# The recurrent block of layer 1 moved ahead of its memory attention, with two sets of gate buffers and a rearranged block loop

## The reference, cut to what matters

```python
def lru_mixer(h, w_in, conv_w, conv_b, wa, ba, wx, bx, lam):
    p = h @ w_in
    xb, gate, mq = jnp.split(p, [LRU_WIDTH, 2 * LRU_WIDTH], axis=-1)
    xc = centred_depthwise_conv(xb, conv_w, conv_b)
    y = (rg_lru(xc, wa[0], ba[0], wx[0], bx[0], lam[0], False)
         + rg_lru(xc, wa[1], ba[1], wx[1], bx[1], lam[1], True))
    y = y * jax.nn.gelu(gate)
    return y, mq.reshape(B, S, MEM_HEADS, MEM_HEAD_DIM)

def rg_lru(x, wa, ba, wx, bx, lam, reverse):
    r = jax.nn.sigmoid(block_diag_linear(x, wa, ba).astype(jnp.float32))
    i = jax.nn.sigmoid(block_diag_linear(x, wx, bx).astype(jnp.float32))
    log_a = -LRU_C * r * jax.nn.softplus(-lam.astype(jnp.float32))
    a = jnp.exp(log_a)
    u = jnp.sqrt(-jnp.expm1(2.0 * log_a)) * (i * xf)
    _, h = lax.associative_scan(_linear_combine, (a, u), axis=1, reverse=reverse)
```

## Time and profile before

| engine | busy us | share of the span |
|---|---|---|
| PE (matmul) | 3663.4 | 91% |
| DVE | 1690.4 | 42% |
| POOL | 1210.8 | 30% |
| ACT | 974.2 | 24% |

### The profile page before, as it was taken

How to read it: one execution, slowest core, us unless ns; L and a number is a source line. 1 busy time by engine, 2 the same in 40 slices (tenths; PEclk the granted TensorE clock), 3 DMA queues, 4 the chain that set the end, 5 groups by cost and what they waited for, 6 DMA issues and landing times. The chain is left out here.

```text
span 4028.1 us, 45875 instructions
## 1 busy us (share of the span) xinstructions
PE 3663.4 (91%) x16526; PEld 2930.9 (73%) x16526; DVE 1690.4 (42%) x1834; ACT 974.2 (24%) x1547; POOL 1210.8 (30%) x650
## 2 busy tenths in 40 slices
PE   6788887999999997977579999999799999978999
PEld 4666665888888885755358888888568888856877
DVE  4324445163343345356634434333643343243454
ACT  2224444020101012343412110101143433312101
POOL 0111002233333331145543333333233443412350
PEclk9899998999999998988789999999899999989999
DMA  3100000221111112011012111111121111111332
GB/s 138 60 21 17 15 11 6 94 68 47 47 51 48 47 47 73 24 34 31 26 68 68 47 47 47 51 47 47 43 73 58 57 42 52 58 40 34 99 102 97
DMA packets 56409, 209.92 MB, mean 52 GB/s; under 512 B 6000, under 2 KB 10352, under 8 KB 55424
## 3 DMA queue, kind: packets, MB, share of 16 engines
q1 hardware_dynamic: 46352, 158.35, 12.8%
q10 hardware_dynamic: 9968, 50.43, 3.3%
HBM read 186.74 MB, written 22.02 MB: 52 GB/s over the span
## 5 line engine op out<-in xcount | busy, mean ns | idle before, releaser
L486 PE MATMUL G<-Hhi,whi 128*128 128x512 f32 x2752 | 1143.3, 415 | 96.5 <-ACT T L1015 33.2
L486 PE MATMUL G<-Hlo,whi 128*128 128x512 f32 x2752 | 1084.1, 394 | 0.0
L486 PE MATMUL G<-Hhi,wlo 128*128 128x512 f32 x2752 | 1083.6, 394 | 0.0
L358 POOL CAST whi<-wraw 128x1024 fp32r<-128x1024 f32 (+1 forms) x268 | 285.5, 1065 | 2465.7 <-PE G L486 1274.3
L486 PEld LDWEIGHTS G<-Hhi,whi 128*128 128x128 f32 x2752 | 524.7, 191 | 238.9 <-issue 87.4
L360 POOL TENSOR_TENSOR wlo<-wraw,whi 128x1024 fp32r<-128x1024 f32 (+1 forms) x268 | 665.3, 2482 | 21.5
L486 PEld LDWEIGHTS G<-Hlo,whi 128*128 128x128 f32 x2752 | 525.1, 191 | 118.7 <-issue 7.4
L486 PEld LDWEIGHTS G<-Hhi,wlo 128*128 128x128 f32 x2752 | 523.6, 190 | 112.0
L486 PE MATMUL G<-Uhi,whi 128*128 128x512 f32 x1024 | 398.8, 389 | 0.0
L486 PE MATMUL G<-Ulo,whi 128*128 128x512 f32 x1024 | 398.8, 389 | 0.0
L486 PE MATMUL G<-Uhi,wlo 128*128 128x512 f32 x1024 | 398.8, 389 | 0.0
(11 more groups left out here) (285 smaller groups left out, 4605.9 us busy)
## 6 DMA issues: line engine op xcount, KB each, us to landing
wraw<-wjobs SPq DMA_DIRECT2D x292, 512.0 KB, 3.5
X<-xT ACTq DMA_DIRECT2D x2, 4096.0 KB, 14.9
scratch<-X ACTq DMA_DIRECT2D x2, 4096.0 KB, 11.9
gate_tiles<-gate_st ACTq DMA_DIRECT2D x16, 512.0 KB, 2.7
T<-gate_tiles ACTq DMA_DIRECT2D x16, 512.0 KB, 3.3
X<-scratch ACTq DMA_DIRECT2D x1, 4096.0 KB, 13.2
X<-scratch SPq DMA_DIRECT2D x4, 1024.0 KB, 11.6
out<-yn ACTq DMA_DIRECT2D x8, 512.0 KB, 2.6
```

The costliest lines, as they stand in the source:

```text
L358: pool.tensor_copy(whi[:, par, 0:kt], wraw[:, par, 0:kt]).then_inc(w_hi, 1)
L486: mm = pe.matmul(G[:, par, cols], w[:, par, k, :], x[:, k, cols], start=(k == 0 and j == 0), stop=(k == kt - 1 and j == 2))
```

## The change

- The phases are reordered: the 16 jobs `lru` come first, then the 4 jobs `mq1`. `lru()` is called before `mem_attention(1)` on PE, ACT and DVE, and the weights lie in memory in that order.
- `rg` and `ig` exist twice (by the parity of the block). The gelu is written straight into `mixed`; `gl` is gone. `a*a` is no longer a square: ACT makes it by a second exponential with twice the constant (`decay_c[:, 96:112]`) into the tiles `lt`, one of which is `T[:, 1]`. So ACT has six activations of a whole tile per block there instead of four.
- POOL does no part of the recurrence any more: `ig * xc` goes to DVE, the square to ACT. POOL's list holds only weight splits through layer 1's mixer; `split_mixed` of six tiles comes after the last `mq1` job.
- ACT's block j: the second direction's sigmoids and the exponentials of block j-1, the gelu of j, the roots of j-1, the first direction's sigmoids of j, the copy of the input of j+1. DVE's block j: convolution of j, then the rest of j-1 (`behind`). PE's block j: job 2j+1, first gates of j, job 2j+2, second gates of j.
- In the last memory head, 12 of the 16 parts of the first `wo_mixed1` job are put between the attention's instructions. The four heads of layer 1 are written out instead of looped, and use `probs1` for `probs`.
- The six `split_mixed` wait for the end of all `mq1` jobs, since they overwrite `Hhi` and `Hlo`.

```diff
@@ PHASES
-    PHASES += [(f"mq{_l}", 4, "act")]
-    PHASES += [("k", 2, "act"), ("v", 2, "act"), ("q", 8, "act")] if _l == 0 else [("lru", 16, "act")]
+    PHASES += [("mq0", 4, "act"), ("k", 2, "act"), ("v", 2, "act"), ("q", 8, "act")] if _l == 0 else \
+              [("lru", 16, "act"), ("mq1", 4, "act")]
@@ POOL
-            splits(START["up00"], START["lru"] + 4)
+            splits(START["up00"], START["lru"] + 2)
...
-                for dr in range(2):
-                    pool.wait_ge(l_sig, j * 4 + (2 * dr + 2))
-                    pool.tensor_tensor(ig[:, dr], ig[:, dr], xc[par][:], ALU.mult).then_inc(l_ix, 1)
-                for dr in range(2):
-                    pool.wait_ge(l_exp, j * 4 + (2 * dr + 2))
-                    pool.tensor_tensor(T[:, dr], av[:, dr], av[:, dr], ALU.mult).then_inc(l_a2, 1)
...
+            splits(START["lru"] + 2, START["wo_mixed1"] + 2)
             pool.wait_ge(job_done, START["wo_mixed1"])
-            for k in range(3):
-                split_mixed(1, k, l_y, k + 1)
-            lru_block(7, 1, last=True)
-            for k in range(3, EARLY):
-                split_mixed(1, k, l_y, k + 1)
+            for k in range(EARLY):
+                split_mixed(1, k, l_y, 2 + k + 1)
@@ PE, mem_attention: the parts between in the last head
+                        if last:
+                            for q in range(max(2 * u - 4, 0), max(2 * u - 2, 0)):
+                                next_part(q, after, 1 - par, shift, (early_lo, EARLY * l))
@@ PE, lru
+                def block_of(j, i, par, ahead=True):
+                    for q in range(16):
+                        next_part(q, j * 2 + (START["lru"] + 1), 1, shift)
                     pe.wait_ge(l_xc, j + 1)
-                    pe.wait_ge(lw_in[par], lw_count * 16 + 16)
+                    pe.wait_ge(lw_in[par], i * 16 + 16)
+                    pe.wait_ge(l_sig, j * 4 + 4)
                     gates(par, 0)
...
+                            next_part(q, j * 2 + (START["lru"] + 2), 0, shift)
+                    pe.wait_ge(l_sig, j * 4 + 6)
+                    gates(par, 1)
@@ ACT, lru
+                def block_of(j, par, jm1, j1, j2):
+                    if jm1 is not None:
+                        sigmoids(jm1, 1 - par, 1)
+                        decays(jm1, 1 - par)
+                    gelu(j)
+                    if jm1 is not None:
+                        roots(jm1)
+                    sigmoids(j, par, 0)
+                    if j1 is not None:
+                        input_of(j1, 1 - par)
@@ DVE, lru
+                def behind(j, par, between=None):
+                    r, i = rg[par], ig[par]
+                    dve.wait_ge(l_sig, j * 4 + 8)
+                    for dr in range(2):
+                        dve.tensor_tensor(i[:, dr], i[:, dr], xc[par][:], ALU.mult).then_inc(l_ix, 1)
+                    for dr in range(2):
+                        dve.wait_ge(l_exp, j * 6 + (3 * dr + 3))
+                        dve.scalar_tensor_tensor(lt[dr][:], lt[dr][:], 1.0, r[:, dr], ALU.add, ALU.mult).then_inc(l_e, 1)
...
+                def block_of(j, par, jm1, x_ahead=True, g_ahead=True):
+                    convolve(j, par)
+                    behind(jm1, 1 - par)
```

More of the change, by code:

```diff
@@ L690, in project_out, with ready @@
             def project_out(l):
-                jobs(f"wo_mixed{l}", 8, Hhi, Hlo,
-                     lambda k: (early_lo, EARLY * l + k + 1) if k < EARLY else (split_lo[l], k - EARLY + 1))
+                name = f"wo_mixed{l}"
+                def ready(k):
+                    return (early_lo, EARLY * l + k + 1) if k < EARLY else (split_lo[l], k - EARLY + 1)
+                if l:
+                    for q in range(12, 16):
+                        job_part(q, START[name], 0, Hhi, Hlo, ready)
+                    psum_waits(name, 1, 1)
+                    job(START[name] + 1, 1, Hhi, Hlo, ready)
+                    with pe.Fori(1, 4) as i:
+                        for par in range(2):
+                            psum_waits(name, i * 2 + par, par)
+                            job(i * 2 + (START[name] + par), par, Hhi, Hlo, ready)
+                else:
+                    jobs(name, 8, Hhi, Hlo, ready)
                 jobs(f"wo_mem{l}", 8, MOhi, MOlo, (split_lo[l], KT - EARLY), kt=4)
@@ L733, in gates @@
                     mm.then_inc(l_mm, 1)
-                def first_gates(j, lw_count, par):
+                def block_of(j, i, par, ahead=True):
+                    for q in range(16):
+                        next_part(q, j * 2 + (START["lru"] + 1), 1, shift)
                     pe.wait_ge(l_xc, j + 1)
-                    pe.wait_ge(lw_in[par], lw_count * 16 + 16)
+                    pe.wait_ge(lw_in[par], i * 16 + 16)
+                    pe.wait_ge(l_sig, j * 4 + 4)
                     gates(par, 0)
[L740 to L745, removed]
                     if ahead:
                         for q in range(16):
[L748 to L755, removed]
+                            next_part(q, j * 2 + (START["lru"] + 2), 0, shift)
+                    pe.wait_ge(l_sig, j * 4 + 6)
+                    gates(par, 1)
+                psum_waits("lru", 0, 0)
+                job(START["lru"], 0, Hhi, Hlo, (norm_s["lo"], tiles_before("nmix1")))
+                pe.wait_ge(evac["dve"], 2 + BASE["lru"]["dve"])
                 with pe.Fori(0, 3) as i:
@@ L758, in lru @@
                         block_of(i * 2 + par, i, par)
-                block_of(6, 3, 0, ahead=False)
-                pe.wait_ge(l_sig, 30)
-                gates(1, 1)
+                block_of(6, 3, 0)
+                block_of(7, 3, 1, ahead=False)
             def gla():
@@ L1169, in input_of, with sigmoids @@
                     act.dma_start(lw[:, par], block).then_inc(lw_in[par], 16)
[L1171 to L1181, removed]
+                def sigmoids(j, par, dr):
+                    if dr == 0:
+                        act.wait_ge(l_y, j + 1)
+                    wait_apart(act, l_mm, j * 2 + (dr + 1))
+                    for g, (dst, b) in enumerate(((rg[par], "lru_ba"), (ig[par], "lru_bx"))):
+                        act.activation(dst[:, dr], AUX[:, 2 * g:2 * g + 2, :].rearrange("p a n -> p (a n)"),
+                                       ACT.Sigmoid, bias=dcol(b, j + 8 * dr)).then_inc(l_sig, 1)
@@ L1186, in block_of, with roots @@
+                def roots(j):
                     for dr in range(2):
                         act.wait_ge(l_e, j * 2 + (dr + 1))
-                        act.activation(T[:, dr], T[:, dr], ACT.Sqrt, scale=-1.0).then_inc(l_sq, 1)
-                    act.wait_ge(l_y, j + 1)
-                input_of(0, 0)
-                with act.Fori(0, 3) as i:
-                    for par in range(2):
-                        block_of(i * 2 + par, par)
-                block_of(6, 0)
-                block_of(7, 1, last=True)
+                        act.activation(lt[dr][:], lt[dr][:], ACT.Sqrt, scale=-1.0).then_inc(l_sq, 1)
@@ new lines, in gelu @@
+                def gelu(j):
+                    wait_apart(act, job_done, j * 2 + (L0 + 2))
+                    act.activation(tile_of(mixed, j), G[:, 1, :], ACT.Gelu_apprx_tanh).then_inc(evac["act"], 1)
+                def block_of(j, par, jm1, j1, j2):
[8 more added lines that the diff above has]
+                        input_of(j1, 1 - par)
@@ new lines, in lru @@
+                act.wait_ge(l_dx, 3)
+                input_of(0, 0)
+                block_of(0, 0, None, 1, True)
+                with act.Fori(0, 2) as i:
+                    block_of(i * 2 + 1, 1, i * 2, i * 2 + 2, True)
+                    block_of(i * 2 + 2, 0, i * 2 + 1, i * 2 + 3, True)
+                block_of(5, 1, 4, 6, True)
+                block_of(6, 0, 5, 7, False)
+                block_of(7, 1, 6, None, False)
+                sigmoids(7, 1, 1)
+                decays(7, 1)
@@ L1198, in gla @@
+                roots(7)
             def gla():
```

120 lines of the change are left out of this document (66 added, 54 removed).

## The result

Four runs of the changed kernel took 3914.3, 3917.45, 3920.78 and 3920.93 us, the median 3919.11; four of the kernel before beside them 4026.27 to 4029.1, the median 4028.41. The ratio is 0.9728, 95% interval 0.9711 to 0.9745: 109 us or 2.7% faster. The forecast was 3911.0, with a range of 3893 to 3945. The profiled run took 3920.78 us, its span is 3919.0.

A forecast was written before the change was run, and what follows sets the result against it. Waits among PE, ACT and DVE held the recurrence; seven periods shortened by 14.2 us (about 99), plus three POOL waits and two lone jobs, less the new open end, saved 117 us: 3911 us, range 3893 to 3945.

The forecast's parts named there:

- Period 29.0: One recurrence block takes 29.0 us, PE's own two jobs and two gates, instead of 43.2 us.
- DVE's 3 to 4 us idle before the roots: Sign in the recurrence blocks: DVE has about 3 to 4 us idle before the roots.
- The sums behind it: Work per recurrence block on other engines: DVE 24.6 us with two POOL splits, ACT 21.4 us with table loads.
- Step 1: Stage start: decay constants stand before the first copy, convolution ends at 1591, costing PE nothing to 1 us.
- step 4: Block 7, no job ahead: PE waits 5.6 us, gates cost up to 6.5, then a stall of 2.2.
- Steps 2 and 3: Block 0's gates and job end at 1609.1; blocks 1 to 6, 29.0 us each, end at 1783.1.
- Step 5: First memory job ends at 1822.8; first head's maximum, queued behind block 7 on DVE, is 5.7 us late at 1834.8.
- Step 6: Attention up to the last splits: 105.7 us plus 5.7 late, less 0.7 at the last head, reaching 1933.5.
- DVE as bound: Rival, 17%: DVE sets the recurrence period; 33 us gives 3939, the upper bound of 37.5 gives 3971.
- POOL late: Rival, 9%: in the last head PE waits 14 us for POOL's six splits, giving 3925 us.
- No overlap: Rival, 4%: recurrence blocks stay chained through ACT, the period stays near 43 us, giving 4010 us.
- The clock: Rival, 3%: PE gets the lower clock level over the stage, its work doubles, giving about 4210 us.

The follow-up runs named there:

- Chained_blocks: Changed kernel, but ACT waits for the last multiply of block j-1 before the gelu of block j: 3980.09 us, 0.9889 of the kernel before.
- Early_constants: Changed kernel, but DVE works out the decay constants in layer 0, long before the stage: 3906.72 us, 0.9706 of the kernel before.
- Second_job_first: Changed kernel, but PE runs memory job 0 before block 7's last gates and memory job 1 whole before head 0: 3911.71 us, 0.9719.

## Why the prediction was right, step by step

It named the mechanism and came within 8 us. On its own clock, from the first job's end to the last splits, it had 353.9 us and the profile has 359.3 (1940.78 less 1581.5, the end that POOL's mark at 1581.61 shows).

- *Period 29.0.* Right: 28.66, PE with no wait. Seven times 0.34 is 2 us on the other side. DVE's 3 to 4 us idle before the roots are 4.3 to 4.5. Chained_blocks shows that the overlap makes this. The sums behind it were too high: DVE is busy 20.8 us a block, not 24.6, so the splits cost it 1.6 us and not 5.4; ACT has 14 tiles a block and not 15, 19.8 us in all with the loads where I had 21.4.
- *Step 1, the step that failed.* "This costs PE nothing to 1 us": it cost 6.2 us of wait and 3.0 of slow gates, 9.2 us. I had taken the constants from a place with no POOL beside the earlier trace rows, 7.1 us with the table load, and a clean convolution of 4.7. Both overlapped a split: the constants end 10.1 us after they began (2.7 of it in the two slowed instructions), the convolution takes 7.4 with its first operation. And the lower level on gates behind a wait was in the earlier trace rows, but I priced it in step 4 only. Early_constants shows that the constants in front make the lateness: with them away, 9.4 us go, though the convolution still ran beside a split. What the splits alone add, 5.3 us, is read from the rows; no run takes them away.
- *Steps 2 and 3.* Right, with the two terms above.
- *Step 4.* The wait of 5.6 us is 5.8, the gates of 6.5 are 5.95, the stall of 2.2 is 2.3.
- *Step 5.* The memory job takes 12.6 us, not 10.9, since it too starts at the lower level. The first maximum is 10.2 us behind its job, not 12.0; DVE's part of block 7 ends 9.8 us after that longer job, with one split beside it, as assumed. Second_job_first shows that DVE's list binds here.
- *Step 6.* From that job to the last splits 108.4 us against 110.7: POOL's splits cost 2.0 us of waits, the size I set; the rest of the difference lies in the later ending of the memory job, behind which less was left for DVE.
- *The rivals.* DVE as bound: not in this kernel, by the windows; the run with four more products is where it becomes so. POOL late: 2.0 us of waits, not 14. No overlap: no, and chained_blocks gives what it would be, near 60 us and not 99. So the 99 us that I put on the shorter period are not the overlap's alone. The clock: 1.00 in the blocks.

That is 9.2 late in step 1 and 1.7 in the memory job, less 2.3 in step 6 and 3.2 in the periods and small terms: 5.4 us. With 1.9 us ahead of the stage (the mark at the first job's end lies between 1574.63 and 1582.82 in the profiles of the versions that leave layer 0 alone) and 0.5 behind the last splits, scatter of executions, that makes the 8 us between 3911 and 3919.

The Trainium skill has the mechanism of step 1 ("SBUF — State Buffer", section "Who interferes with whom"): a DVE instruction with two SBUF inputs contends with a GpSimd instruction that reads SBUF, and the shared ports are an exclusive lock. The rows agree to a tenth of a us: a product of 128x16, 0.17 us elsewhere, started at 1583.06 under POOL's subtraction of 1582.73 to 1585.14, and ended at 1585.18; the memset before it, which reads nothing, took its 0.07 us under the same subtraction. I had used the rule as a sum per block; what I missed is that a small instruction pays as much as a large one, here the rest of the subtraction. For the table loads the Trainium skill ("ScalarE: Activation LUTs", section "What ACT_TABLE_LOAD costs") with its drain behind every load would have made it 3917, nearer than my 3911; but the activation still stands 0.01 to 0.02 us behind a load of 1.28 in the blocks (load at 1718.84, root at 1720.14), so it would be right for a reason that the trace denies.

## What to carry to other kernels

Where a change turns a chain into a pipeline, the period is easy to forecast and the error sits at the two ends: walk through the first and the last turn instruction by instruction, with every neighbour that is running there, a POOL split above all. Charge each wait of PE of some us with the slow matmuls behind it. And look for setup work that depends on nothing (here 30 small instructions) standing in front of the pipeline's first turn.

## What was not expected of the hardware

- Gates behind a wait of PE of over 5 us took 5.15 to 6.7 us for the same eight matmuls that take 3.59 otherwise; behind 1.0 to 1.5 us 3.70. Between, the length of the wait alone does not tell: 5.39 behind 2.50 us in one block with four products, 3.70 behind 3.56 us in the last with eight. In the chained kernel the mean granted clock over 1648 to 1868 is 0.90, where it is 1.00 without the waits: a wait of 5.5 us cost 8.2.
- A Pool product beside DVE: 3.4 us there, and 2.0 us more on each DVE operation beside it. Work given to POOL cost DVE more time than doing it itself (22.3 us a block against 20.8).
- Parts of a job laid into the last head filled no wait there on balance: with them the head took 23.3 us (1914.19 to 1937.44), without them 15.2 (1909.60 to 1924.77), and the 12 parts are 36 matmuls of 0.228 us, 8.2 us. PE's idle time in the head was 3.6 us with them and 3.5 without, as the small waits that they filled came back as 1.9 us of waits for POOL's splits. PE then stood still for 2.85 and 3.47 us behind the head, with nothing left to run.
